# Decoder block on one core: the moving operand of the 512 column products read as four interleaved runs

## The reference

```python
proj = einsum('bsd,de->bse', x, w_in) 
q, k, v, cb, cc, ch, g_conv, g_attn = split(proj)
y_conv = cb * causal_conv3(cc * ch)
y_attn = sliding_window_attention(q, k, v, sinks)    # 16 heads on 4 key heads, window 128, ALiBi, sink
merged = sigmoid(g_conv) * y_conv + sigmoid(g_attn) * y_attn
x = layer_norm(ALPHA * x + merged @ w_out, ln1_g, ln1_b)
hid = silu(x @ w_gate) * (x @ w_up)                  # 2816 wide
x = layer_norm(ALPHA * x + hid @ w_down, ln2_g, ln2_b)
```

## Time and profile before

| what | before |
|---|---|
| median of 3 executions | 1456.26 us |
| lowest and highest | 1455.56 and 1458.51 us |
| the profiled execution's own time | 1455.48 us |
| span of the profile (first to last instruction) | 1453.6 us |
| PE matmuls | 1436.0 us busy, 99% of the span |
| DVE | 796.9 us busy, 55% |
| POOL | 601.7 us busy, 41% |
| ACT | 485.3 us busy, 33% |

### The profile page before, as it was taken

One profiled execution on the slowest core, in us unless ns is written; L12 is line 12 of the kernel. 1 busy time (PEld: TensorE's weight loads), 2 busy tenths in 40 slices (PEclk: granted clock), 3 DMA queues, 4 the chain that ended last, 5 costly groups with the idle time before them and its releaser, 6 DMA issues. The chain is left out here.

```text
span 1453.6 us, 19033 instructions
## 1 busy us (share of the span) xinstructions
PE 1436.0 (99%) x6658; PEld 1193.9 (82%) x6658; DVE 796.9 (55%) x1196; ACT 485.3 (33%) x933; POOL 601.7 (41%) x374
## 2 busy tenths in 40 slices
PE   9999999999999999999999999999999999999997
PEld 8888888888888888887887788888888888888886
DVE  3126664566357743767867835535345453454547
ACT  4433433333234423434245332322323223232133
POOL 2212122212212131124873483754737547464464
PEclk9999999999999999999999999999999999999999
DMA  5211111111111011111420121112111112121112
GB/s 174 59 44 44 41 33 55 32 43 43 43 43 43 29 44 46 41 44 59 121 83 15 58 74 44 58 44 65 51 42 58 51 58 65 29 64 59 44 51 116
DMA packets 128406, 80.22 MB, mean 55 GB/s; under 512 B 8432, under 2 KB 123120, under 8 KB 128368
## 3 DMA queue, kind: packets, MB, share of 16 engines
q1 hardware_dynamic: 128368, 79.73, 18.2%
HBM read 75.53 MB, written 4.19 MB: 55 GB/s over the span
## 5 line engine op out<-in xcount | busy, mean ns | idle before, releaser
L476 POOL TENSOR_TENSOR w_lo<-raw,w_hi 128x1024 fp32r<-128x1024 f32 x54 | 131.7, 2439 | 507.2 <-ACT w_hi L616 507.2
L1353 PE MATMUL ps<-act_hi,w_hi 128*128 128x512 f32 x864 | 338.6, 392 | 1.2 <-DVE act_lo L913 1.2
L1355 PE MATMUL ps<-act_hi,w_lo 128*128 128x512 f32 x864 | 336.6, 390 | 0.0
L1354 PE MATMUL ps<-act_lo,w_hi 128*128 128x512 f32 x864 | 336.5, 390 | 0.0
L564 POOL TENSOR_TENSOR w_lo<-raw,w_hi 128x512 fp32r<-128x512 f32 x80 | 108.5, 1356 | 227.7 <-ACT w_hi L826 227.7
L1355 PEld LDWEIGHTS ps<-act_hi,w_lo 128*128 128x128 f32 x864 | 162.2, 188 | 34.4
L1353 PEld LDWEIGHTS ps<-act_hi,w_hi 128*128 128x128 f32 x864 | 162.3, 188 | 33.5 <-issue 1.4
L1354 PEld LDWEIGHTS ps<-act_lo,w_hi 128*128 128x128 f32 x864 | 162.4, 188 | 32.0
L1353 PE MATMUL ps<-hid_hi,wd_hi 128*128 128x512 f32 x320 | 124.9, 390 | 3.4 <-DVE res L1192 3.4
L1198 DVE TENSOR_TENSOR res<-res,ps 128x512 f32<-128x512 f32 x128 | 87.9, 687 | 68.3 <-PE ps L1355 67.7
L1354 PE MATMUL ps<-hid_lo,wd_hi 128*128 128x512 f32 x320 | 124.5, 389 | 0.0
(11 more groups left out here) (193 smaller groups left out, 2548.0 us busy)
## 6 DMA issues: line engine op xcount, KB each, us to landing
raw<-in_w_in SPq DMA_DIRECT2D x52, 512.0 KB, 3.8
raw_d<-in_w_down SPq DMA_DIRECT2D x22, 512.0 KB, 3.3
raw<-in_w_gate SPq DMA_DIRECT2D x40, 256.0 KB, 2.9
raw<-in_w_up SPq DMA_DIRECT2D x40, 256.0 KB, 3.2
raw<-in_w_out SPq DMA_DIRECT2D x16, 512.0 KB, 3.6
xs<-in_x SPq DMA_DIRECT2D x8, 512.0 KB, 8.1
out<-rows SPq DMA_DIRECT2D x7, 512.0 KB, 2.6
raw_b<-in_w_gate SPq DMA_DIRECT2D x1, 512.0 KB, 5.3
```

The lines of the kernel that those rows point to most:

```text
L476: pool.tensor_tensor(w_lo[:, slot], raw[:, slot], fp(w_hi[:, slot]), ALU.subtract).then_inc(w_lo_s, 1)
L1353: pe.matmul(bank, w_h(t), a_hi(t), start=(t == 0), stop=False)
L1354: pe.matmul(bank, w_h(t), a_lo(t), start=False, stop=False)
L1355: last = pe.matmul(bank, w_l(t), a_hi(t), start=False, stop=(t == tiles - 1))
```

## The change

Two helpers give another view of the same memory. `folded` takes 512 contiguous elements as 128 groups of four, where the four lie 128 elements apart: the order of reading is 0, 128, 256, 384, 1, 129, ... Every matmul of `product`, `pair_product` and the values is given its moving operand in this order. Token 128 a + b so lands in word 4 b + a of its bank. `bank_of` is the inverse view of a bank: words 0, 4, 8, ... are the first 128 tokens, and so on. `tokens` cuts the other operands and the result of an instruction that empties a bank into four runs of 128, so that shapes agree; their memory order stays. The matmuls of `last_rows`, the scores, the transposes and the statistics stay as they are. No instruction is added, removed or moved; the number and the order of instructions on each engine are the same.

```diff
+        def folded(ap):
+
+            return ap.rearrange("p (a b) -> p b a", a=4)
+
+        def tokens(ap):
+
+            return ap.rearrange("p (a b) -> p a b", a=4)
+
+        def bank_of(b):
+
+            return ps[:, b, :].rearrange("p (b a) -> p a b", a=4)
...
-                act.activation(u_st[:, 0], ps[:, BX, :], ACT.Copy).then_inc(s1_s, 1)
+                act.activation(tokens(u_st[:, 0]), bank_of(BX), ACT.Copy).then_inc(s1_s, 1)
...
-                    o_ps = ps[0:HD, OUT, :].rearrange("p (j e q) -> p e j q", j=2, e=2)
-                    lo = o_lo[:].rearrange("p (j e q) -> p e j q", j=2, e=2)
+                    o_ps = ps[0:HD, OUT, :].rearrange("p (q j e) -> p e j q", j=2, e=2)
+                    lo = o_lo[:].rearrange("p (q j e) -> p e j q", j=2, e=2)
...
-                    dve.tensor_tensor(tile, tile, ps[:, 4 + v % 4, :], ALU.add).then_inc(add_s, 1)
+                    dve.tensor_tensor(tile, tile, bank, ALU.add).then_inc(add_s, 1)
...
-                x, y, z, w = (ps[:, b, :] for b in (BX, BY, BZ, BW))
+                x, y, z, w = (bank_of(b) for b in (BX, BY, BZ, BW))
...
-                    pe.matmul(bank, w_h(t), a_hi(t), start=(t == 0), stop=False)
-                    pe.matmul(bank, w_h(t), a_lo(t), start=False, stop=False)
-                    last = pe.matmul(bank, w_l(t), a_hi(t), start=False, stop=(t == tiles - 1))
+                    hi, lo = folded(a_hi(t)), folded(a_lo(t))
+                    pe.matmul(bank, w_h(t), hi, start=(t == 0), stop=False)
+                    pe.matmul(bank, w_h(t), lo, start=False, stop=False)
+                    last = pe.matmul(bank, w_l(t), hi, start=False, stop=(t == tiles - 1))
...
-                                last = pe.matmul(ps[:, OUT, :], vs[:, n - 1 + kb, :], part[:, kb],
+                                last = pe.matmul(ps[:, OUT, :], vs[:, n - 1 + kb, :], folded(part[:, kb]),
...
-                    b_hi, b_lo = right(j, t)
+                    b_hi, b_lo = (folded(ap) for ap in right(j, t))
```

More of the change, by code:

```diff
@@ L631, in _ @@
                 act.wait_ge(unit_s, n + 1)
-                bank = ps[:, unit_bank(n + 1), :]
+                bank = bank_of(unit_bank(n + 1))
                 if t < 2:
@@ L635, in _ @@
                         act.wait_ge(v_turned, n - 1)
-                    act.activation(yc[:, half(n % 2)], bank, ACT.Copy).then_inc(v_copied, 1)
+                    act.activation(tokens(yc[:, half(n % 2)]), bank, ACT.Copy).then_inc(v_copied, 1)
                 else:
@@ L641, in _ @@
                         for to in range(2):
-                            act.activation(res[to * HD:(to + 1) * HD, 2 * (2 * j + e), half(h)],
-                                           bank[e * HD:(e + 1) * HD, :], ACT.Copy).then_inc(k_copied, 1)
+                            act.activation(tokens(res[to * HD:(to + 1) * HD, 2 * (2 * j + e), half(h)]),
+                                           bank[e * HD:(e + 1) * HD], ACT.Copy).then_inc(k_copied, 1)
                 if (t, h) in ((0, 1), (1, 1), (2, 1)):
@@ L660, in _ @@
                         h = n % 2
-                        bank = ps[:, unit_bank(n), :]
+                        bank = bank_of(unit_bank(n))
                         done = k * (2 * NT) + (2 * PRO_TILES + n + 1)
@@ L668, in _ @@
                                 rows = slice(e * HD, (e + 1) * HD)
-                                act.activation(q_st[rows, 2 * j + e, half(h)], bank[rows, :],
+                                act.activation(tokens(q_st[rows, 2 * j + e, half(h)]), bank[rows],
                                                ACT.Copy).then_inc(q_hi_s, 1)
                         elif kind == "ga":
-                            act.activation(tga[:, j, half(h)], bank, ACT.Tanh, scale=0.5).then_inc(ga_s, 1)
+                            act.activation(tokens(tga[:, j, half(h)]), bank, ACT.Tanh, scale=0.5).then_inc(ga_s, 1)
                         elif kind == "cc":
@@ L675, in _ @@
                                 act.wait_ge(conv_s, k * 24 + 12)
-                            act.activation(ccs[:, half(h)], bank, ACT.Copy).then_inc(cc_s, 1)
+                            act.activation(tokens(ccs[:, half(h)]), bank, ACT.Copy).then_inc(cc_s, 1)
                         elif kind == "gc":
@@ L679, in _ @@
                                 act.wait_ge(conv_s, k * 24 + 10)
-                            act.activation(tgc[:, half(h)], bank, ACT.Tanh, scale=0.5).then_inc(gc_s, 1)
+                            act.activation(tokens(tgc[:, half(h)]), bank, ACT.Tanh, scale=0.5).then_inc(gc_s, 1)
                         if h == 1 and n < 2 * NT - 1:
@@ L770, in silu_tanh @@
                     act.wait_ge(hid_s, 3 * t + 1)
-                act.activation(t_g[:, t], ps[:, 2 * t, :], ACT.Tanh, scale=0.5).then_inc(silu_s, 1)
+                act.activation(tokens(t_g[:, t]), bank_of(2 * t), ACT.Tanh, scale=0.5).then_inc(silu_s, 1)
             def silu_high(h, t):
@@ L838, in gate_tanh @@
                     act.wait_ge(pair_s, i * 48 + (STEPS_OF * c + LOW0))
-                    act.activation(t_g[:, 0], ps[:, BX, :], ACT.Tanh, scale=0.5).then_inc(tanh_s, 1)
+                    act.activation(tokens(t_g[:, 0]), bank_of(BX), ACT.Tanh, scale=0.5).then_inc(tanh_s, 1)
                 else:
@@ L966, in unit @@
                             dve.wait_ge(q_hi_s, k * 8 + (4 * j + 2 * h + 2))
-                            dve.tensor_tensor(q_st[other, 2 * j + e, cols], bank[rows, :],
-                                              fp(q_st[rows, 2 * j + e, cols]), ALU.subtract).then_inc(q_lo_s, 1)
+                            dve.tensor_tensor(tokens(q_st[other, 2 * j + e, cols]), bank[rows],
+                                              tokens(fp(q_st[rows, 2 * j + e, cols])), ALU.subtract).then_inc(q_lo_s, 1)
                     elif kind == "ch":
@@ L973, in unit @@
                         conv_done(j, 4 * h)
-                        dve.tensor_tensor(u_pad[:, 2 + h * HALF:2 + (h + 1) * HALF], bank, ccs[:, cols],
+                        dve.tensor_tensor(tokens(u_pad[:, 2 + h * HALF:2 + (h + 1) * HALF]), bank, tokens(ccs[:, cols]),
                                           ALU.mult).then_inc(conv_s, 1)
@@ L993, in unit @@
                         conv_done(j, 10 + h)
-                        dve.tensor_tensor(res[:, bass.ds(k * 2 + j, 1), cols].rearrange("p a s -> p (a s)"), bank,
-                                          yc[:, cols], ALU.mult).then_inc(conv_s, 1)
+                        dve.tensor_tensor(tokens(res[:, bass.ds(k * 2 + j, 1), cols].rearrange("p a s -> p (a s)")), bank,
+                                          tokens(yc[:, cols]), ALU.mult).then_inc(conv_s, 1)
                 def soft_done(n, step):
@@ L1121, in _ @@
                 dve.wait_ge(xsum_s, DT * 2 if h else 2 * m + 1)
-                dve.scalar_tensor_tensor(out=res[:, m, half(h)], in0=res[:, m, half(h)], scalar=ALPHA,
-                                         in1=ps[:, out_bank(v), :], op0=ALU.mult, op1=ALU.add).then_inc(res_s, 1)
+                tile = tokens(res[:, m, half(h)])
+                dve.scalar_tensor_tensor(out=tile, in0=tile, scalar=ALPHA,
+                                         in1=bank_of(out_bank(v)), op0=ALU.mult, op1=ALU.add).then_inc(res_s, 1)
                 if h == 0:
@@ L1143, in hidden_up @@
                 dve.wait_ge(hid_s, 6 * h + 3 * t + 1)
[L1144 removed]
+                dve.tensor_tensor(tokens(u_st[:, t]), tokens(u_st[:, t]), bank_of(2 * t + 1), ALU.mult).then_inc(hid_s, 1)
             def hidden_low(h, t):
@@ L1188, in add_down @@
                 h, m = v // DT, v % DT
-                tile = res[:, m, half(h)]
+                tile, bank = tokens(res[:, m, half(h)]), bank_of(4 + v % 4)
                 dve.wait_ge(d_s, i * 32 + (16 * c + v + 1))
                 if how == "first":
-                    dve.scalar_tensor_tensor(out=tile, in0=tile, scalar=ALPHA, in1=ps[:, 4 + v % 4, :], op0=ALU.mult,
+                    dve.scalar_tensor_tensor(out=tile, in0=tile, scalar=ALPHA, in1=bank, op0=ALU.mult,
                                              op1=ALU.add).then_inc(add_s, 1)
                 elif how == "biased":
-                    dve.scalar_tensor_tensor(out=tile, in0=tile, scalar=alpha_b[:, m:m + 1], in1=ps[:, 4 + v % 4, :],
+                    dve.scalar_tensor_tensor(out=tile, in0=tile, scalar=alpha_b[:, m:m + 1], in1=bank,
                                              op0=ALU.add, op1=ALU.add).then_inc(add_s, 1)
                 else:
-                    dve.tensor_tensor(tile, tile, ps[:, 4 + v % 4, :], ALU.add).then_inc(add_s, 1)
+                    dve.tensor_tensor(tile, tile, bank, ALU.add).then_inc(add_s, 1)
             dve.tensor_scalar(alpha_b[:], lnb[:], ALPHA, None, ALU.mult).then_inc(ab_s, 1)
@@ L1252, in pair @@
                 product_done(THIRD_DIFF)
[L1253 removed]
+                dve.tensor_tensor(up, u1, y, ALU.add).then_inc(pair_s, 1)
                 done(U3)
[L1255 removed]
```

(8 more changed lines are left out.)

5 lines of the change are left out of this document (3 added, 2 removed).

## The result

The changed kernel takes 1745.01 us (median of 4, 1743.1 to 1745.72) against 1455.91 us before, a ratio of 1.198 (95% interval 1.1959 to 1.2001). It is slower by 289 us, where + 1244 was forecast.

What follows compares the result with a forecast made beforehand. PE was taken to bound the kernel, through 5832 matmuls at 226.7 ns. A further 213.3 ns each made + 1244 us on 1455.5, so 2700 us; likeliest case 2622 to 2780, range for 8 in 10 from 1452 up.

Steps and rivals of the forecast that it cites:

- The bound: Whole kernel: PE busy 1436.0 of 1453.6 us, the 5832 touched matmuls at 226.7 ns making 1322 us of it.
- The term that failed: PE's moving reads: a fetch for each scattered column, 0.833 ns in place of 0.42, + 1244 us in all; chance 0.53.
- the 440: Folded matmuls in dense stretches: 440.0 ns each forecast between starts, in place of 226.7.
- the rival without any change of rate: PE's moving reads: several fetched pieces held at once, so the matmul price stays; 1455.5 us, chance 0.13.
- my reading: PE's moving reads: a fetch comes once per 0.83 ns and brings neighbours, two of which are used; an inference.
- one hit per line: PE's moving reads: by the skill's rule of two accesses per 16 byte line the new order is penalised, no price given.
- the partial price: PE's moving reads: some fetches overlap, between 5 and 180 ns a matmul, 1485 to 2505 us; chance 0.08.
- The late banks: Down stretches: stepped bank reads cost ACT and DVE twice, PE waits 0 to 4 us in each; 1475 us, chance 0.07.
- The faster rival: Start of each matmul: scattered order avoids a clash with the weight load, up to 78 us saved, 1378 us; chance 0.14.
- the 13.3 ns: Each 512-column matmul: the fixed part of 226.7 ns beyond 213.3 ns for the columns at 2.4 GHz.
- The clock: PE: could fall if it waits for data, but at 1.2 GHz a column also takes 0.833 ns, so no term.
- the two main cases: PE's moving reads: double column price (0.53) or no change of rate (0.13), 1244 us apart, nothing likely between.

Runs made afterwards that it cites:

- e1: The changed kernel with the banks read word by word, so only PE's order of reading differs from the kernel before: 1743.38 us, ratio 1.1972.
- e2: The kernel before with only the banks read in steps of four words, PE reading 512 contiguous columns: 1456.76 us, ratio 1.0004.
- the grids: Runs of the kernel before with many orders of reading PE's moving operand, one per product; between 216 and 526 ns from matmul to matmul, no kernel time given.
- e8: Kernel before, eleven more orders on a fixed tile, four runs with middle two exchanged: 129 apart 234 natural, 274 exchanged; 130 apart 276 and 230 ns.
- e4: Kernel before with fewer weight columns in a hidden tile's seven products: contiguous 231, 230, 229 ns at 32, 64, 128; four runs 275 to 283 ns.
- e6: The changed kernel with two interleaved runs in place of four and banks emptied in steps of two: 1405.26 us, ratio to before 0.9645.

## Why the prediction was wrong

**The bound: right.** PE was and is the bound, 5832 matmuls carry the difference, e1 gives all of it and e2 none, and the products that are not folded kept their time.

**The term that failed** is this one: "Scattered columns then need a fetch each, and the column price goes to 0.833 ns." It made 213.3 ns a matmul; measured are 46 to 57 ns. Times near the 440 that I had worked out exist, but for other orders: one run in steps of two to four elements costs 450 to 460 ns and eight runs 442 to 494. Four runs do not pay that price for each column. The reading that the grids support is that what is fetched stays: the next column of the same run, four columns later, is served from the line already held. I had seen this ("PE may hold several fetched pieces at once") and filed it as the rival without any change of rate, since I took holding the lines to be enough.

**What takes its place.** The reading that fits the orders of the four runs with grids, and that e8 was made to test, is this. Even and odd columns go through two readers, each with a few lines of 16 bytes. A new line now and then is free; a reader that needs one in two of its steps running loses time. With two runs each reader walks through one run and needs a line every fourth step: 216 ns. Contiguous reading gives each reader every other element, a new line every second step: 227 to 236, and two runs in steps of two do the same to each reader and take 229. With four runs 128 apart each reader alternates between two runs that cross their borders together, two new lines in two steps running, 32 times a matmul: (283 - 216) / 32 = 2.1 ns each time, 1.8 ns at 273. In steps of two to four elements every step of one run needs a line: 450 and more. With eight runs 64 or 128 apart each reader has four lines to keep and does worse than that, so it keeps fewer than four; with six runs it has three, and 305 ns are far from 450, so by the model it keeps three. The words "reader" and "line" are a model; shown are the distances. The model says which orders are dear, and not how dear: 2.1 ns for each second new line in four runs, but (451 - 216) / 255 = 0.9 ns where every step needs one, and nothing in it tells 434 from 526 ns at sixteen runs. The surplus of four runs over two grows with the columns: 25, 41 and 67 ns at 256, 384 and 512.

The rule that I had set beside my reading (the Trainium skill, SBUF — State Buffer, the section on Door 1: 16 byte lines, at least two accesses to the same line) is borne out in part. Its line size agrees with the pieces of four, 237 and 451 ns. Its two hits do not agree as the Trainium skill words them, as consecutive accesses. One run in steps of two elements has two hits in a row in every line, and so have the pieces of two, and they took 452 and 451 ns; two interleaved runs have none in a row and took 216. Counted for each reader by itself, two hits do fit: two runs in steps of two elements give two and took 229 ns, one run in steps of two gives one and took 452. My sentence that the new order has "one hit per line" left out that each line gets four hits, one in every fourth column.

**The rivals.** What happened is the partial price, to which I gave 0.08, with 50 ns within its 5 to 180; it had no mechanism beyond "some of the fetches overlap". The late banks did not come: DVE's adds kept their 0.69 us (e2), and PE waits for no `res` any more. The faster rival was right in one thing, that part of the 13.3 ns of contiguous reading can be had back by another order: 10.9 ns of it, with two runs. Its cause is not borne out: a narrower weight load gives nothing back (e4). The Trainium skill's figure of 215.7 ns for 512 columns, which I had cited beside the trace's 226.7 (TensorE: Matmul & The Clock Gate, the section "Wait — 56ns, not 53.3ns?"), is what two runs reach, with 215.8. The clock stayed high and was rightly left out of the sum.

**The range** held 1745, but was too wide to say much, and that it did was no merit of the mechanism; and of the two main cases "nothing lies likely between them" was the wrong sentence, as it rested on a mechanism with only two outcomes.

**Still open:** why the same order costs 273 ns in one stage and 283 in another; why four runs 129 or 131 apart take 230 to 235 ns and not the 216 of two runs, though each reader needs a new line as often; and what contiguous reading loses to two runs, which is 11 ns at 512 columns, 12 at 384 (184 against 172) and 7 at 256 (119 against 112), so neither the same for every matmul nor in proportion to the columns.

## What to carry to other kernels

Where matmuls of fp32r stand 227 ns apart at 512 columns, let the moving operand come from two interleaved runs and read the bank back in steps of two: 216 ns here, and 3.5% of a kernel that PE bounds. Emptying the banks cost no more (the adds kept 686 ns); the one sum with an SBUF operand in steps went from 413 to 446 ns. Try a new access pattern in one product first, since two, four and eight runs differ by a factor of two, and a grid of patterns fits into one run. When a price is bounded by two distant ends, ask what mechanism would land between them before calling the middle unlikely.

## What the runs showed of the hardware that I had not expected

- Contiguous is not the fastest order for PE's moving operand: 226.7 ns for 512 contiguous fp32r columns, 216 for two interleaved runs at each of ten distances from 1 to 1024 elements.
- Where an operand starts may matter a little: 227, 236, 232 and 229 ns for contiguous reading from element 0, 1, 2 and 3 of a tile. As reading from element 0 took up to 231 ns in other places, only the 236 stands clear.
- DVE reads a bank in steps of four words without loss (686 ns for 512 elements), but when an SBUF operand comes in steps too, 256 elements take 413 ns contiguous, 446 in steps of two (e6, a mean of 407 to 509) and 608 in steps of four (e2):

```profile
L1048 DVE TENSOR_TENSOR o_sum<-ps,o_lo 64x256 f32<-64x256 f32 x64 | 28.5, 446 | 3.9 <-ACT o_lo L713 2.9
```
